# Seven half products for the output projection of a decoder block, in place of eight

## The reference

```python
h = _rmsnorm(x, norm_mix[l])
merged = (jax.nn.sigmoid(g_sb) * (o_sb @ w_branch_sb[l])
          + jax.nn.sigmoid(g_sa) * (o_sa @ w_branch_sa[l]))
x = x + merged @ w_out[l]
h2 = _rmsnorm(x, norm_mlp[l])
x = x + jnp.square(jax.nn.relu(h2 @ w_ff1[l])) @ w_ff2[l]
```

## Time and profile before

| | |
|---|---|
| three runs | 726.17, 727.34, 725.69 us |
| median | 726.17 us |
| span of the profiled execution | 724.9 us |
| TensorE busy | 716.9 us |
| VectorE busy | 537.2 us |
| ScalarE busy | 341.9 us |
| GpSimd busy | 259.6 us |
| granted TensorE clock, mean | 1.000 |

### The profile page before, as it was taken

How to read it: one execution, slowest core, us unless ns; L and a number is a source line. 1 busy time by engine, 2 the same in 40 slices (tenths; PEclk the granted TensorE clock), 3 DMA queues, 4 the chain that set the end, 5 groups by cost and what they waited for, 6 DMA issues and landing times.

```text
span 724.9 us, 9771 instructions
## 1 busy us (share of the span) xinstructions
PE 716.9 (99%) x3454; PEld 575.0 (79%) x3454; DVE 537.2 (74%) x771; ACT 341.9 (47%) x492; POOL 259.6 (36%) x207
## 2 busy tenths in 40 slices
PE   8999999999999899999999999999999999999998
PEld 5878878787776666788888988888888888888887
DVE  7354889899886875537646569695968869595898
ACT  6244753365567777722324353624335253624441
POOL 2104325001223564003301080725427090725677
PEclk9999999999999999999999999999999999999999
DMA  9308231311110212133190235141330605131103
GB/s 331 142 15 252 97 115 60 117 59 59 59 59 23 51 45 59 59 117 117 32 345 1 65 110 175 59 168 64 114 118 17 213 1 174 58 116 58 59 1 117
DMA packets 44039, 70.65 MB, mean 97 GB/s; under 512 B 2657, under 2 KB 27489, under 8 KB 44002
## 3 DMA queue, kind: packets, MB, share of 16 engines
q1 hardware_dynamic: 44000, 70.16, 29.6%
q10 hardware_dynamic: 2, 0.00, 0.0%
HBM read 65.71 MB, written 2.10 MB: 94 GB/s over the span
## 4 chain that ended last, share of the span: by engine, by line
PE 94%; DVE 2%; POOL 1%; ACT 1%; issue 1%; DMA 0%; DVEq 0%; ACTq 0%
PE ps L1950 8%; PE ps L1951 8%; PE ps L1952 8%; PE ps L1979 7%; PE ps L1980 7%; PE ps L1981 7%; PE ps L436 6%; PE ps L438 6%; PE ps L437 6%; PE ps L429 6%; PE ps L431 6%; PE ps L430 6%; PE ps L1861 1%; PE ps L1755 1%; PE ps L1871 1%; PE ps L1789 1%
## 5 line engine op out<-in xcount | busy, mean ns | idle before, releaser
L1950 PE MATMUL ps<-b_hi,cut_hi 128*128 128x512 f32 (+1 forms) x280 | 104.1, 372 | 0.0
L1951 PE MATMUL ps<-b_lo,cut_hi 128*128 128x512 f32 (+1 forms) x280 | 103.8, 371 | 0.0
L1952 PE MATMUL ps<-b_hi,cut_lo 128*128 128x512 f32 (+1 forms) x280 | 103.8, 371 | 0.0
L653 POOL TENSOR_TENSOR a_lo<-qo_sb,a_hi 128x512 fp32r<-128x512 f32 x56 | 91.8, 1666 | 14.2 <-ACT a_hi L976 14.2
L436 PE MATMUL ps<-cut_hi,a_hi 128*128 128x512 f32 x216 | 86.4, 400 | 0.0
L438 PE MATMUL ps<-cut_hi,a_lo 128*128 128x512 f32 x216 | 84.5, 391 | 0.0
L437 PE MATMUL ps<-cut_lo,a_hi 128*128 128x512 f32 x216 | 84.3, 390 | 0.0
L965 ACT ACTIVATE qo_sb<-ps 128x512 f32<-128x512 f32 x32 | 19.2, 599 | 130.3 <-PE ps L1952 86.3
L420 DVE TENSOR_TENSOR cut_lo<-raw,cut_hi 128x2048 fp32r<-128x2048 f32 (+2 forms) x33 | 51.2, 1551 | 27.5 <-ACT cut_hi L412 27.4
L661 POOL TENSOR_TENSOR qo_sb<-qo_sb 128x512 f32<-128x512 f32 x7 | 9.1, 1295 | 154.0 <-DVE qo_sb L1409 154.0
L412 ACT ACTIVATE cut_hi<-raw 128x2048 fp32r<-128x2048 f32 (+2 forms) x33 | 48.5, 1470 | 31.1 <-PE ps L431 22.7
(11 more groups left out here) (218 smaller groups left out, 1652.3 us busy)
## 6 DMA issues: line engine op xcount, KB each, us to landing
raw<-in_w_ff_dram SPq DMA_DIRECT2D x32, 1024.0 KB, 5.5
raw<-in_w_in_dram SPq DMA_DIRECT2D x16, 1024.0 KB, 5.8
gates<-in_x_dram SPq DMA_DIRECT2D x8, 512.0 KB, 5.5
raw<-in_w_out_dram SPq DMA_DIRECT2D x4, 1024.0 KB, 5.1
raw<-in_w_in_dram SPq DMA_DIRECT2D x4, 512.0 KB, 6.9
raw<-in_w_branch_sb_dram SPq DMA_DIRECT2D x2, 1024.0 KB, 5.1
raw<-in_w_branch_sa_dram SPq DMA_DIRECT2D x4, 512.0 KB, 6.9
out_dram<-gates SPq DMA_DIRECT2D x7, 256.0 KB, 2.1
```

The source lines that it names most:

```text
L1950: T.matmul(dst, w_hi[:, w], b_hi[:, k, a:b], start=(k == 0), stop=False)
L1951: T.matmul(dst, w_hi[:, w], b_lo[:, k, a:b], start=False, stop=False)
L1952: mm = T.matmul(dst, w_lo[:, w], b_hi[:, k, a:b], start=False, stop=(k == KD - 1))
```

## The change

The output projection becomes Strassen's scheme in the form with shared sums. With the token halves `old` (tokens 0 to 255) and `new` (256 to 511) and the depth halves, `merged` has the blocks m11, m12, m21, m22, and `w_out` the blocks w11, w21, w12, w22, one slab each. Seven products of 24 matmuls (`out_product`) take the place of eight:

- sums of `merged`, on POOL: S3 = m11 - m21, S1 = m21 + m22, S2 = S1 - m11, S4 = m12 - S2, each 1024 columns, and their low parts, also on POOL (`out_sum_low`);
- sums of weights, on DVE: wt1 = w12 - w11, wt3 = w22 - w12, wt2 = w22 - wt1, wt4 = w21 - wt2, each 2048 columns; low parts of seven right operands on DVE (`out_weight_low`) in place of four;
- `merged` now lies in `qo_sb`, not in `gates`; of its first four tiles only the new tokens are cut;
- TensorE's order is A11, S3, A22, S2, S1, A12, S4, two token tiles t each, written x.t here. Only A11, S3 and A12 start a bank; the others accumulate onto a product that has been added to `xres` already, so they wait for that addition (`wo_out`);
- 14 additions to `xres` in place of 8 (`X_ADDS`); tokens 256 to 511 are whole after S4. The turns of tiles 0 and 1 lie in A12, that of tile 2 after the first block of half-width MLP matmuls, where it stood ahead of it;
- the loads of `x`, the gain and the first MLP weights have other waits and another order on SP.

```diff
+O_TURN = [O_A11, O_S3, O_A22, O_S2, O_S1, O_A12, O_S4]
+O_CUTS = [O_A11, O_S3, O_A22, O_S2, O_A12, O_S1, O_S4]
+O_BANK = {O_A11: 0, O_S2: 0, O_S1: 0, O_S4: 0, O_S3: 2, O_A22: 2, O_A12: 6}
+X_ADDS = [(O_S3, 0, 1), (O_A11, 2, 0), (O_A22, 0, 0), (O_S2, 0, 0), (O_S1, 0, 1), (O_A12, 2, 0), (O_S4, 2, 1)]
...
-            for m in range(TB):
-                sp.wait_ge(mg_cut, 4 * (m // 2) + 4)
...
+            sp.wait_ge(mg_sum, 4)
+            load_x(1)
+            sp.wait_ge(os_lo, O_SUMS.index(O_S3) + 1)
+            load_x(0)
...
+            sp.wait_ge(mg_sum, 8)
+            load_x(2)
+            load_x(3)
...
+            for f in range(4):
+                merge(f)
+            pool.wait_ge(mg_sum, 4)
+            pool.tensor_tensor(osum[O_S3], m11, m21, ALU.subtract).then_inc(os_made, 1)
+            out_sum_low(O_S3)
+            for f in range(4, 8):
+                merge(f)
+            pool.wait_ge(mg_sum, 8)
+            pool.tensor_tensor(osum[O_S1], m21, m22, ALU.add).then_inc(os_made, 1)
+            pool.wait_ge(os_made, 2)
+            pool.tensor_tensor(osum[O_S2], osum[O_S1], m11, ALU.subtract).then_inc(os_made, 1)
+            out_sum_low(O_S2)
+            out_sum_low(O_S1)
+            pool.wait_ge(os_made, 3)
+            pool.wait_ge(ow_lo, O_CUTS.index(O_A22) + 1)
+            pool.tensor_tensor(osum[O_S4], m12, osum[O_S2], ALU.subtract).then_inc(os_made, 1)
+            out_sum_low(O_S4)
...
+            def add_to_x(q, t):
+                n = [a for a, _, _ in X_ADDS].index(q)
+                m, half = X_ADDS[n][1] + t, X_ADDS[n][2]
+                dve.wait_ge(op_done, out_end(q) - 1 + t)
+                if q in (O_S3, O_A11):
+                    dve.wait_ge(x2_in[m], 16)
...
+            for t in range(2):
+                add_to_x(O_S3, t)
+            out_weight_low(O_S2)
+            for t in range(2):
+                add_to_x(O_A11, t)
+            out_weight_low(O_A12)
+            for t in range(2):
+                add_to_x(O_A22, t)
+            out_weight_low(O_S1)
+            for t in range(2):
+                add_to_x(O_S2, t)
+            out_weight_low(O_S4)
+            for t in range(2):
+                add_to_x(O_S1, t)
...
-            slab_ready(SL_OUT)
-            pe.wait_ge(br_out, 12)
-            for m in range(TB):
-                mm = out_part(0, 0, m)
...
+            def out_product(q, turned=None):
+                w_hi, w_lo = o_home[q]
+                l_hi, l_lo = o_left[q]
+                pe.wait_ge(ow_lo, O_CUTS.index(q) + 1)
+                if q in O_SUMS:
+                    pe.wait_ge(os_lo, O_SUMS.index(q) + 1)
+                else:
+                    pe.wait_ge(mg_cut, 4 if q == O_A11 else 8)
+                opens = q in (O_A11, O_S3, O_A12)
+                for t in range(2):
+                    if q == O_A12:
+                        pe.wait_ge(br_out, 16)
+                    elif opens:
+                        pe.wait_ge(br_out, 12)
+                    else:
+                        pe.wait_ge(wo_out, added({O_A22: O_S3, O_S2: O_A11, O_S1: O_S2, O_S4: O_S1}[q]) - 1 + t)
...
             pe.wait_ge(nt_cut, 12)
+            pe.wait_ge(wo_out, added(O_A12))
             ff1_part(0, 0, 0, 256)
+            norm_turn(TB + 2, xn2[0])
             ff1_part(0, 1, 0, 256)
```

More of the change, by code:

```diff
@@ L380, in slab_used @@
                 return gate_done, 2 * (i - SL_GATE) + 2
[L381 to L384, removed]
+            return br_done, 4 * (i - SL_BR) + 4
         def ff_arrived(j, g):
@@ L1351, in add_to_x, with out_weight_low @@
[L1351 to L1356, removed]
-                dve.wait_ge(x2_in[m], 16)
-                dve.wait_ge(wo_done, m + 1)
-                add_to_x(0, m).then_inc(wo_out, 1)
-            dve_cut(SL_OUT + 3)
+            def out_weight_low(q):
+                dve.wait_ge(ow_hi, O_CUTS.index(q) + 1)
+                hi, lo = o_home[q]
+                V.tensor_tensor(lo, o_right[q], hi.bitcast(F32), ALU.subtract).then_inc(ow_lo, 1)
@@ new lines, in gated, with merged_low @@
+            def gated(q, j):
+                f = 8 * (q % 2) + 4 * (q // 2) + j
+                dve.wait_ge(br_done, 4 * q + j + 1)
+                V.tensor_tensor(gates[:, f, :], bank(4 * (q % 2) + j), gates[:, f, :], ALU.mult).then_inc(br_out, 1)
+            def merged_low(f):
+                t = new if f < 4 else slice(0, S)
+                dve.wait_ge(mg_hi, f + 1)
+                V.tensor_tensor(a_lo[:, f, t], merged[:, f, t], a_hi[:, f, t].bitcast(F32), ALU.subtract).then_inc(mg_cut, 1)
@@ new lines, in _ @@
+            dve_cut(SL_BR + 1)
+            out_weight_low(O_A11)
+            dve_cut(SL_BR + 2)
+            dve.wait_ge(gsb_ready, 8)
+            for j in range(4):
+                gated(0, j)
+            dve_cut(SL_BR + 3)
+            dve.wait_ge(gsa_ready, 4)
+            for j in range(4):
+                gated(1, j)
+            dve.wait_ge(*slab_arrived(SL_OUT + 2))
+            V.tensor_tensor(wt1, w12, w11, ALU.subtract).then_inc(ot_made, 1)
+            for f in range(4):
+                merged_low(f)
@@ new lines, in _ @@
+            dve.wait_ge(*slab_arrived(SL_OUT + 3))
+            V.tensor_tensor(wt3, w22, w12, ALU.subtract).then_inc(ot_made, 1)
+            dve.wait_ge(ot_made, 1)
+            V.tensor_tensor(wt2, w22, wt1, ALU.subtract).then_inc(ot_made, 1)
+            for j in range(4):
+                gated(2, j)
+            dve.wait_ge(gsa_ready, 8)
+            gated(3, 0)
+            gated(3, 1)
+            out_weight_low(O_S3)
+            gated(3, 2)
+            gated(3, 3)
+            dve.wait_ge(*slab_arrived(SL_OUT + 1))
@@ new lines, in _ @@
+            dve.wait_ge(ot_made, 3)
+            dve.wait_ge(mg_sum, 4)
+            V.tensor_tensor(wt4, w21, wt2, ALU.subtract).then_inc(ot_made, 1)
+            for f in range(4, 8):
+                merged_low(f)
+            out_weight_low(O_A22)
+            def add_to_x(q, t):
[4 more added lines that the diff above has]
+                    dve.wait_ge(x2_in[m], 16)
+                elif q != O_S4 and q != O_A22:
+                    dve.wait_ge(wo_out, added({O_S2: O_A22, O_S1: O_S3, O_A12: O_A11}[q]) - 1 + t)
+                part = xres[:, m, half * 512:(half + 1) * 512]
+                V.tensor_tensor(part, bank(O_BANK[q] + t), part, ALU.add).then_inc(wo_out, 1)
@@ L1572, in dve_last @@
                 drain(g, A22, last=True)
[L1574 removed]
+            dve.wait_ge(wo_out, added(O_S4))
             dve_round(0, first=True)
@@ L1911, in _ @@
                     mm.then_inc(br_done, 1)
-            def out_part(n, half, m):
-                for k in range(4):
-                    kk, t = 4 * half + k, slice(m * P, (m + 1) * P)
-                    if n == 0 and m == 0:
-                        pe.wait_ge(mg_cut, kk + 1)
-                    mm = moving_weights(SL_OUT + 2 * n + half, k, bank(m), a_hi[:, kk, t], a_lo[:, kk, t],
-                                        start=(kk == 0), stop=(kk == 7))
-                return mm
-            slab_ready(SL_OUT)
@@ L1944, in ff1_part @@
+            for q in O_TURN:
+                out_product(q, (0, 1) if q == O_A12 else None)
             def ff1_part(n, c, a, b, into=None):
@@ L1996, in _ @@
             ff1(0, 3)
-            pe.wait_ge(wo_out, 8)
+            pe.wait_ge(wo_out, added(O_S4))
             def pe_round(g, first=False):
```

216 lines of the change are left out of this document (127 added, 89 removed).

## The result

| | before | after |
|---|---|---|
| median of the runs | 725.93 us (725.42 to 727.34) | 737.64 us (736.71 to 738.11) |
| ratio, 95% interval | | 1.0159 (1.0147 to 1.0170) |
| span of the profiled run | 724.9 us | 735.0 us |
| first branch matmul to last matmul | 419.0 us | 429.3 us |
| in that stretch, less than before: 24 matmuls | | -5.4 us |

What follows compares the result with a forecast made beforehand. TensorE, busy 99% of the span, was taken as the bound. Removing 5.4 us and adding stalls of 3.3, 8.9, 2.7 and 1.5 gave +10.7 step by step; with +0.4 for the clock, 737.3 us, range 732.0 to 742.5.

Steps and rivals of the forecast that it cites:

- Removed work: Output projection on TensorE: seven products of 24 matmuls replace 192 matmuls, 24 fewer at 0.2267 us each, 5.4 us removed.
- Stall 1: Ahead of the first product, A11: its PSUM banks are freed late, behind VectorE's weight sums and low parts; 3.3 us.
- Stall 2: Ahead of the third product, A22: A22.0 must wait for VectorE's addition S3.0, queued behind sums and low parts; 8.9 us.
- Stall 3: Ahead of product S1: the addition S2.0 stands behind the low parts of S2, A12 and S1; 2.7 us.
- Stall 4: At the norm of the third tile: rows 256 to 511 are whole only after S4, the last product; 1.5 us.
- Clock: TensorE's clock falling after stall 2: only A22.0 at half speed, 2.7 us more, nearly all absorbed by stall 3; +0.4 us.
- a rival: Clock falls for long: both halves of A22 and a group after stalls 1 or 3 at half speed; 740 to 742.5, chance 0.15.
- the dearer case: At A22, after stall 2: A22.1 also runs at half clock, not only A22.0; +3.2 us in place of +0.4.
- The GpSimd form: GpSimd's 1024-column operation, priced between 2.32 and 2.59 us from other rows; 2.4 us taken.
- the turns: GpSimd and SBUF-only VectorE operations wait for each other, whole instruction for whole instruction, so durations add; 733 to 740 us, 0.69.
- no turns: Rival in the output projection: sums slip into VectorE's gaps and stalls 1 to 3 vanish; -3.9, 722.3 us, chance 0.06.
- partial turns: Rival: only merging sums hold VectorE; stall 2 shrinks to 3.8, stalls 1 and 3 go; 726 us, up to 733, chance 0.06.

Runs made afterwards that it cites:

- experiment 5: The kernel after, with 24 bf16 matmuls of 512 columns into unused bank 4 ahead of product A22, keeping TensorE busy in its longest wait: 735.9 us.
- experiment 3: The kernel after with the same instructions on the same engines, only VectorE's queue reordered so that gated multiplications follow their products: 726.18 us, ratio 0.9998 of before.
- experiment 9: The kernel before, with eight further GpSimd additions of 1024 columns whose result nobody reads: 727.84 us, ratio 1.0027 of before.
- experiment 2: The kernel after, with VectorE's four weight sums (wt1, wt3, wt2, wt4) cut from 2048 columns to 64, their low parts still whole: 726.5 us.

## Why the prediction was right, and where not

The time, 737.3 us, is 0.3 from what was measured, and the account behind it is made of the right pieces. That it is so near is partly luck: the sizes of the pieces were off by up to 3.7 us and cancelled.

- **Removed work**, -5.4: the 24 instructions are gone and the groups of 12 still take 2.72 us. Right.
- **Stall 1**, ahead of A11: 3.3 forecast, 2.9 measured, released by the gated operation named. Right, though the terms shown there (331.6 + 10.3 + 7.8 = 349.7, less 346.6) give 3.1.
- **Stall 2**, ahead of A22: 8.9 forecast, 6.5 measured, released by the addition S3.0. The place and the queue were right, the size 2.4 too large. S3.1 was over at 360.96 (I had 360.8), the addition started at 366.67 (I had 369.0, in a count in which the branch began 1.3 us later: 303.01 before, 301.69 after). On that footing VectorE was 1.0 us earlier than counted, and A11's half at low clock made TensorE 1.5 us later.
- **Stall 3**, ahead of S1: 2.7 forecast, none measured. A22.0 at half clock had used it up. With A22.0 at full clock a wait of 2.1 us stands there (experiment 5).
- **Stall 4**, at the turns: 1.5 forecast, 1.2 + 0.2 measured. Right, and untouched by turns and sums: 1.2 us in every kernel with the old order of the last additions.
- **Clock**: +0.4 forecast. The slow matmuls cost 4.1 in the account, of which 1.7 at A11 and 2.3 at A22. This is the term that was mis-sized. I let only A22.0 fall and hid that in stall 3, which is as it came; but TensorE was already at half clock behind the 2.9 us ahead of A11, which the prediction gave only to a rival. The Trainium skill ("TensorE: Matmul & The Clock Gate", Part 1) has an idle engine fall to 1.2 GHz and return with sustained work, and the trace agrees with the fall: behind both waits the rows last 0.63 us in place of 0.39. That both halves of A22 would be slow was my own reading: of A22 only 10 matmuls of 24 were. So the dearer case didn't come, and the cheap one left out what A11 paid.
- **In sum** the four stalls came to 16.4 forecast and 10.8 measured, the clock was 3.7 too small, the latencies at the gaps (0.5) were left to the range, and following the steps one by one had taken off 0.3. That makes 11.1 forecast and 10.2 measured in the stretch; what the medians have over it no step had.
- **The GpSimd form** not in the trace: 2.4 taken; 2.42 measured with VectorE reading only PSUM (a low part, L701 at 373.31 in experiment 3), 2.46 for the sum L710. Right.

**The cause.** The prediction called the turns the point that decides, with the rivals "no turns" and "partial turns" as the only faster ones. The durations it named were seen (4.50 for wt2, 3.92 for the low part), and experiment 9 shows the turns as such. The Trainium skill ("SBUF — State Buffer", section Who interferes with whom) says that a VectorE instruction with two SBUF inputs contends with a GpSimd instruction that reads SBUF, through ports that only one of them can hold. The trace agrees, with 3.98 us for 2.29. But experiment 3 makes the loss good with turns still in place. So the step that said "durations must be *added*" was right; what it took for granted was that the sum then stands in front of TensorE. A distinction was missing: the same work, in an order in which bank-freeing operations don't wait behind sums that are needed later. What is shown: most of the loss needs GpSimd's sums, VectorE's weight sums and the order, all three; changing any one of them brings back 8.2, 11.1 or 11.5 us of 11.7. Moving GpSimd's sums to VectorE without a good order brings back only 3.0.

What stays open: the 1.7 us of experiment 5 by the medians against 0.3 in the stretch, which of the moves of experiment 3 was needed, and the last 3 to 4 us of each span, whose spread I didn't explain.

## What to carry to other kernels

Ahead of a change that trades TensorE work for work on the engines beside it, count the exclusive time of VectorE and GpSimd together per stage, and then ask of every operation in VectorE's queue whom it keeps waiting: put those that free a bank (multiplications out of PSUM, additions to x) right behind their product, and sums needed later behind them. A wait that moves when one operation is moved (2.9 + 6.5 to 9.0) belongs to a queue, not to the place where it is seen. This advice is taken from whole orders; no run tested its parts one by one. Try a new order before taking work away: here it was worth as much as taking away all weight sums.

## What the runs showed of the hardware that I had not expected

- TensorE's clock fell already behind a wait of 2.4 to 2.9 us: 8 matmuls at 0.43 us from start to start in after (2.86 us idle) and in the reordered kernel (2.44 us), 10 behind 6.53 and 7.36 us, but only 6 and 7 behind 9.0 and 3.58 us. So the number of slow matmuls didn't grow with the idle time ahead of them. Part of the time at half clock can pass in the wait itself. In the stage table of after the granted clock is 0.50 from 365.4 on, with the first matmul of A22 only at 367.49:

```profile
361.00:365.40 4.40, 0.00 (x0) 0.00 (x0) 4.40 (x3) 3.07 (x3) 3.15 (x3) 1.00 0.32 128
365.40:372.20 6.80, 4.71 (x11) 3.77 (x12) 6.80 (x6) 4.23 (x3) 6.80 (x2) 0.50 0.00 0
```

- The fall can also come after the restart: in experiment 5 the first five matmuls behind the 2.86 us ahead of A11 ran at full clock and the next eight at half. Behind the waits of 1.40 and 2.06 us there, and of 2.10 us in experiment 2, it had not fallen.
- GpSimd's 1024-column operation took 2.42 and 2.46 us with two different inputs (L701 in experiment 3 at 373.31, L710 in after), and 1.9 us where both inputs were the same tile (experiment 9, three in a row at 1.89, 1.89 and 1.90 us when VectorE was idle or reading PSUM).
